# Both paged caches loaded from the SyncE queue, GpSimd left with the row stores

## The reference

```
x = x + 0.5*g1*SwiGLU_1(mod1(rmsnorm(x)))
h = mod2(rmsnorm(x)); [qA|kA|vA|qB|kB|vB|gA|gB] = h @ w_in
   branch A: block-sparse attention, 8 heads x 64, blocks of 256, top 3 past blocks + own
   branch B: differential attention, 4 heads, q/k halves of 64, value 128
   past k, v of a sample: cache[page_table[s]], 8 pages of 128 tokens x 512 values, per cache
x = x + g2*((sig(gA)*yA + sig(gB)*yB) @ w_out)
x = x + 0.5*g3*SwiGLU_2(mod3(rmsnorm(x)))
outputs: y, and the new key and value rows of both branches
```

## Time and profile before

| | |
|---|---|
| median of 3 runs | 827.73 us (826.56 to 828.61) |
| the profiled execution | 827.75 us |
| its span | 826.0 us |
| PE busy | 743.0 us (90%) |
| DVE busy | 489.2 us (59%) |
| ACT busy | 321.0 us (39%) |
| POOL busy | 82.3 us (10%) |
| bytes moved | 209.53 MB: 172.05 on q1, 36.44 on q0 |

### The profile page before, as it was taken

The page is one execution under the profiler, slowest core; times in us unless marked ns, Lnnn a source line. Parts: engine busy times, 40 slices in busy tenths (PEclk is TensorE's granted clock), DMA queues, the critical chain, the costliest instruction groups (busy, mean ns, idle before and its releaser), DMA issues. The chain is left out here.

```text
span 826.0 us, 16944 instructions
## 1 busy us (share of the span) xinstructions
PE 743.0 (90%) x6574; PEld 656.3 (79%) x6574; DVE 489.2 (59%) x663; ACT 321.0 (39%) x510; POOL 82.3 (10%) x152
## 2 busy tenths in 40 slices
PE   5589999999999988877778799979897999999997
PEld 2369898989997987767566466749787999999997
DVE  2625444445454899989995534676657545554442
ACT  2434333334333643322304533545335443544341
POOL 0000000000001202433330332300000000000000
PEclk9799999999999997999959999998898999999999
DMA  8978989897666975999993999974342565655530
GB/s 356 373 259 324 302 311 311 304 310 236 195 227 213 371 238 203 378 378 384 380 377 114 371 377 366 337 263 130 125 154 84 171 203 159 197 168 170 184 116 27
DMA packets 132903, 209.53 MB, mean 254 GB/s; under 512 B 6714, under 2 KB 100186, under 8 KB 128738
## 3 DMA queue, kind: packets, MB, share of 16 engines
q1 hardware_dynamic: 121312, 172.05, 61.1%
q0 software_dynamic: 11296, 36.44, 11.9%
q10 hardware_dynamic: 226, 0.10, 0.0%
HBM read 205.31 MB, written 3.24 MB: 253 GB/s over the span
## 5 line engine op out<-in xcount | busy, mean ns | idle before, releaser
L925 DVE TENSOR_TENSOR wlo<-raw,whi 128x1024 fp32r<-128x1024 f32 (+1 forms) x192 | 226.8, 1199 | 211.4 <-ACT whi L639 209.1
L1347 PE MATMUL bank<-hhi,whi 128*128 128x264 f32 x992 | 291.1, 293 | 18.3 <-DVE hlo L972 8.4
L1348 PE MATMUL bank<-hlo,whi 128*128 128x264 f32 x992 | 286.2, 289 | 0.0
L1349 PE MATMUL bank<-hhi,wlo 128*128 128x264 f32 x992 | 285.7, 288 | 0.0
L639 ACT ACTIVATE whi<-raw 128x1024 fp32r<-128x1024 f32 (+1 forms) x192 | 194.9, 1035 | 142.6 <-PE bank L1349 90.4
L1347 PEld LDWEIGHTS bank<-hhi,whi 128*128 128x128 f32 x992 | 192.1, 194 | 32.8 <-issue 21.6
L1348 PEld LDWEIGHTS bank<-hlo,whi 128*128 128x128 f32 x992 | 192.2, 194 | 0.2
L1349 PEld LDWEIGHTS bank<-hhi,wlo 128*128 128x128 f32 x992 | 191.1, 193 | 0.0
L1347 PE MATMUL bank<-ahi,whi 128*128 128x264 f32 x416 | 120.8, 290 | 4.0 <-DVE alo L1319 4.0
L1349 PE MATMUL bank<-ahi,wlo 128*128 128x264 f32 x416 | 119.2, 287 | 0.0
L1348 PE MATMUL bank<-alo,whi 128*128 128x264 f32 x416 | 118.9, 286 | 0.0
(11 more groups left out here) (237 smaller groups left out, 762.9 us busy)
## 6 DMA issues: line engine op xcount, KB each, us to landing
raw<-in_w_ada SPq DMA_DIRECT2D x32, 1024.0 KB, 6.9
raw<-in_ffn_w_gate SPq DMA_DIRECT2D x22, 1024.0 KB, 5.4
raw<-in_ffn_w_up SPq DMA_DIRECT2D x22, 1024.0 KB, 5.4
raw<-in_w_in SPq DMA_DIRECT2D x20, 1024.0 KB, 14.1
raw<-in_ffn_w_down SPq DMA_DIRECT2D x16, 1024.0 KB, 5.4
kvB<-in_cache_k_diff POOLq DMA_DIRECT2D x44, 256.0 KB, 6.6
kvA<-in_cache_k_moba SPq DMA_DIRECT2D x44, 256.0 KB, 9.0
kvA<-in_cache_v_moba SPq DMA_DIRECT2D x44, 256.0 KB, 6.6
```

Of the source, the lines that this page charges most:

```text
L925: dve.tensor_tensor(half_view(wlo[key[1] % 2], key, t), half_view(raw[s], key, t), half_view(whi[key[1] % 2], key, t).bitcast(F32), ALU.su ...
L1347: mm(out, wh, xh, start=start, stop=False)
L1348: mm(out, wh, xl, start=False, stop=False)
L1349: return mm(out, wl, xh, start=False, stop=stop)
```

## The change

SyncE issues the pages of both caches: for each use those of A, then those of B, then the weight tiles that AHEAD puts there. GpSimd keeps only the waits for and the stores of the rows, in the order in which the rows come (KV_BLOCKS: k0, v0, k1, v1, k2, k3, v2, v3). The register reads of `page_ids` are done by SyncE once for A and once for B. ScalarE gets a wait for the stores of all value rows ahead of the second feed-forward block, which overwrites their memory.

```
--- before.py
+++ after.py
@@ -542,14 +542,17 @@
             load_w(W_KV)
             sp.wait_ge(s_gemm, half_done(W_QK - 1, 1))
             for use in range(KVS - 1):
-                kv_load(sp, 0, use)
+                for ab in range(2):
+                    kv_load(sp, ab, use)
             load_w(W_KV + 1)
             load_w(W_KV + 2)
-            kv_load(sp, 0, KVS - 1)
+            for ab in range(2):
+                kv_load(sp, ab, KVS - 1)
             load_w(W_KV + 3)
             load_w(W_KV + 4)
             for use in range(KVS, 4 * TS):
-                kv_load(sp, 0, use)
+                for ab in range(2):
+                    kv_load(sp, ab, use)
                 if use in AHEAD:
                     for n in AHEAD[use]:
                         load_w(n)
@@ -590,9 +593,6 @@
             pool.wait_ge(s_sil, 1)
             pool.dma_start(const[:, late:NCONST], A["consts"][:, late:NCONST]).then_inc(s_const_late, 16)
             pool.wait_ge(s_gemm, half_done(W_QK - 1, 1))
-            pool.wait_ge(s_ptab, 16)
-            for use in range(KVS):
-                kv_load(pool, 1, use)
 
             def row_out(name, ab, p, src, srcs, done):
                 c0 = 256 * p
@@ -608,14 +608,11 @@
             for b in range(2):
                 ins = nc.gpsimd.memset(qrow[b][:, :, :], 0.0)
             ins.then_inc(s_qzero, 1)
-            for use in range(KVS, 4 * TS):
-                kv_load(pool, 1, use)
-                if use in K_ROWS:
-                    i = K_ROWS[use]
+            for kind, i in KV_BLOCKS:
+                if kind == "k":
                     pool.wait_ge(s_tok, 4 * (i + 1))
                     row_out("k", i // 2, i % 2, ktok, ktoks, s_krow)
-                if use in V_ROWS:
-                    i = V_ROWS[use]
+                else:
                     pool.wait_ge(s_vtok, 4 * (i + 1))
                     row_out("v", i // 2, i % 2, vtok, vtoks, s_vrow)
 
@@ -900,6 +897,7 @@
             squares(3, s_xup, 8)
             row_root(2)
 
+            a.wait_ge(s_vrow, 16 * 8)
             nc.scalar.activation(misc[:, 20:21], misc[:, 21:22], ACT.Silu)
             norm_hi(2)
             with a.Fori(0, NPAIR // 2) as i:
```

## The result

The changed kernel takes **838.77 us**, median of 4 runs (835.68 to 839.93), beside 828.06 us for the kernel before (826.56 to 828.61): ratio 1.0135, 95% interval 1.0107 to 1.0164. It is slower by 10.7 us, where 823.2 was forecast with a range up to 831.5. The profiled execution took 839.71 us, its span is 837.9 us, 11.9 more than before. The stages show where they went. The marks are the starts of rows in the timelines (the norm ahead of the projection, VectorE's first and last turn of a key slot, TensorE's first and last value product, VectorE's split of the attention's output, the first weight issue of the second feed-forward block).

A forecast was written before the change was run, and what follows sets the result against it. The prediction saw VectorE and DMA nearly full in the K stage, TensorE and DMA in the V stage, with cache A's pages late. Gains of 8.6 us less 4 for SyncE's pace gave 823.2 us, range 818.8 to 831.5.

The forecast's parts named there:

- what remains if SyncE keeps up: Both attention stages: one queue in order of need removes the stalls at uses 7 and 20, 8.6 us gained together.
- the old stall: V stage: TensorE waits 4.7 us for cache A's value page of use 20, as cache B took half the bandwidth.
- held back by a full queue: K stage: SyncE's four issues of use 7 took 8.56 us behind a weight tile, where free ones take 1.92.
- SyncE's pace: Both stages: SyncE needs 14.1 us per pair of uses, against VectorE's 14.4, DMA's 13.7 and TensorE's 14.0.
- I take it near nothing: Issue slots: a full queue's hold on SyncE, of unknown size up to 8.56 us per slot, costs almost nothing.
- I take the stage as VectorE's again, 2.26 us shorter: K stage: SyncE has some us in hand, so VectorE sets the pace and the stall of use 7 goes.
- its own tipping point of 14.4: K stage: SyncE becomes the bound from about 14.4 us per pair of uses, VectorE's own need.
- The V stage's sum: SyncE's issuing from 448.5 plus 3 us of holds: last page out at 539, landed at 543, 4 us given back.
- SyncE becomes the bound: Rival: the second cache's issue in even uses, behind reads and a weight, makes it slower, 833.1 us; chance 0.15.
- SyncE is the bound and the time is above 827: Sign of being wrong: VectorE waits in the K stage for `kvB` pages again and again.
- no difference: Rival: same bytes and engines, SyncE's pace takes what the order gives; within 2.5 us of 827.7; chance 0.22.
- The parts costed at nothing: ScalarE's new wait covered by 128 us, key-row stores covered by 22.11 us; weight tiles up to 1 us in range.

The follow-up runs named there:

- e1: The changed kernel, but SyncE reads the page numbers once per sample for both caches: 816.46 us, ratio 0.9877 to the kernel before.
- e3: The kernel before, but SyncE issues cache B's value pages while GpSimd keeps its key pages: 832.74 us, ratio 1.0071.
- e6: The changed kernel with the K stage's six weight tiles one use later, behind odd uses: 830.16 us, ratio 1.0027.
- e6b: The kernel of e6 run again, beside c1: 832.23 us, ratio 1.0056.
- e9: The changed kernel with page numbers read once for both caches in the K stage only: 827.53 us, ratio 1.0004.
- e7: e1 with four more page-number reads ahead of the pages of use 31 alone: 827.57 us, ratio 0.9994.
- c1: The changed kernel itself, run again beside e6b: 836.7 us, ratio 1.0105 to the kernel before.
- e4: The kernel before, with SyncE reading the page numbers twice in each even use: 828.66 us, ratio 1.0006.
- e5: The kernel before, with the weight tiles of uses 6 and 19 moved behind uses 7 and 20: 829.13 us, ratio 1.0027.
- e2: The kernel before, but SyncE issues cache B's key pages while GpSimd keeps its value pages: 832.29 us, ratio 1.0059.
- e8: e1 with the K stage's weight tiles behind odd uses: 814.78 us, ratio 0.9822.
- e8b: The kernel of e8 run again, on another chip: 817.77 us, ratio 0.9877.

## Why the prediction was wrong

**The gains were there.** Use 7 and use 20 wait for no page of A in after, and 16 products of use 20 take 2.1 us where they took 3.5. e1, in which SyncE keeps up, sizes them: the K stage is 2.3 us shorter (2.26 was forecast), the V stage 7.4 (4.66 + 1.7 = 6.4). To that comes a gain that the forecast did not have, 1.9 us ahead of the first turn. Altogether 11.7 us of span, 1.1 of them ahead of the second norm where the programs are alike, against the 8.6 of the step "what remains if SyncE keeps up". It doesn't keep up in the kernel as changed: the pages of B for use 20, forecast to be there at 466 to 468, are issued only from 466.58 to 468.60. The forecast's account of the old stall was short as well. It had 6.3 MB to move by 474.5; the windows of before give 257 GB/s in 450 to 460 and 387 in 460 to 475 us, 8.4 MB, so more lay ahead of that page than was counted. And "held back by a full queue" was read into the 8.56 us; no run shows how full the queue was.

**The step that failed is SyncE's pace.** "SyncE then needs 4 x 2.1 + 2 x 2.6 + 0.43 for a weight = 14.1 us", and the hold by a full queue: "I take it near nothing". The pair shown above needs 9.31 us for its four slots (1.88, 1.93 with its gap, 3.56, 1.94), 5.56 for the two reads and 0.64 around the weight: 15.51. A free slot was cheaper than put down (1.9, not 2.1), a read dearer (2.78, not 2.6), and the hold behind the weight, 1.5 us here and 0.7 to 1.8 behind the other five weights, is the term that was left out. Six pairs, from 323.06 to 418.20, average 15.86 us, 1.5 above VectorE's 14.4: 9.24 for the slots, 1.6 more than four free ones, and 6.62 for reads and weight, where 5.63 was forecast. Over six pairs SyncE falls 8.4 us behind its pace in e1 (86.8 us for the same stretch); 6.3 reach VectorE; that the lead of the filled slots takes up the rest is argued, not shown. So "I take the stage as VectorE's again, 2.26 us shorter" became 4.0 longer. The forecast stood only 0.3 us a pair from its own tipping point of 14.4, and a term of unknown size was set to nothing on the favourable side of it: that is the fault, more than the size of any one row.

**The V stage's sum was right in form.** Forecast: start 448.5, 87.5 us of issuing, 3 of holds, last page out at 539, landed at 543. Measured: start 453.40, last page out at 545.76, landed at 552.89. Of the 9.9 us, 4.9 are the late start, nearly all inherited from the K stage, 1.9 the pace, and 3.1 the landing (7.13 us, taken as 4). The three us of holds that were put in here were needed, and were missing one stage earlier.

**A term was missing at the end.** The sum priced late pages of the last use by their lateness alone. TensorE idles for them just ahead of a serial stretch, and from 550 to 560 us its clock is 0.54. That stretch took 15.0 us instead of 9.4 in after, e3, e6, e6b, e9 and e7, and 13.8 in c1, and e7 shows that lateness alone brings it. The 5.6 us are half of the whole loss of 10.7 us. The forecast also had only `kvB` late; 2.90 of the 3.93 us of waiting are for A's page. The prediction had charged a clock cost of 1.7 us behind the stall of use 20, and did not carry the thought to the stall that it forecast itself.

**The rival "SyncE becomes the bound"** is what happened, at the place it named: the second cache's issue in an even use, behind the reads and a weight. Its mechanism of size was not the right one (it had pages at 0.6 us throughout; they are 0.52 and held in places), and its 833.1 lacks the 5.6 us of the end. With them it would have come to 838.7, in part by chance, as its terms were not the measured ones. With VectorE in want of pages again and again, "SyncE is the bound and the time is above 827" read the new profile rightly.

**The page's rule.** The Trainium skill, page "DMA: Bandwidth & Descriptors", section "Issuing engines are not separate DMA queues", was weighed as a reason for no difference. That all DMAs share the same 16 engines fits: q1 alone reaches 380 to 383 GB/s in e1, as both queues did in before. By its second sentence, spreading issues over engines saves only sequencer time, usually small beside the transfer. Here the runs differ on both counts. The spread also decided whose pages came first: e1, with one order, is 11.4 us faster than before. That the order alone brings this is not shown, since e1 also takes the page issues off GpSimd. And the sequencer time was not small, since a 256 KB page costs 0.52 us to issue and 0.35 more for its share of the reads (5.56 us over 16 pages), against 0.68 us to move at 384 GB/s.

**The parts costed at nothing** stayed there: ScalarE's new wait, the key rows (20.90 us of cover where there were 22.11), and the weight tiles, as the stretch behind the attention is 25.8 us long in both kernels. The gain of 1.9 us ahead of the first turn fits ScalarE's waits for `raw<-in_w_in` in the projection, 5.9 us in before and none in after. It goes with the key pages' queue: the stretch is 36.7 to 36.9 us in all four kernels where GpSimd issues B's key pages (before, e3, e4, e5; ScalarE's waits are 6.3 us in e3) and 34.8 to 35.0 in all others. That GpSimd's first pages compete with these tiles is the likely reason; no run shows more than that.

What stays open is how the hold arises. The rows show that slots behind a 1 MB weight tile are issued slowly, and that with a read between it is mostly a later slot that is held; how much a queue takes before it holds the engine was not measured. Nor was it settled why the K stage at SyncE's pace varies so much, 158.4, 161.8 and 163.7 us in after, c1 and e2, where the five executions with the shared read there (e1, e7, e8, e8b, e9) lie within 151.8 to 152.1. Nor is the order of need priced apart from GpSimd's release: no run kept both queues and held B's pages back.

## What to carry to other kernels

Before DMAs are gathered on one engine, add up that engine's own time per period, with register reads and holds, and compare it to the bound; if they meet within a few per cent, the unknown terms decide, so set none of them to nothing. Look for work that the merger doubles but needn't: here one shared read of page numbers turned a loss of 10.7 us into a gain of 11.4. And price a late arrival by what runs behind it: just ahead of a serial stretch of small matmuls, a few us of idle time cost TensorE's clock here, and as much again.

## What the runs showed that was not expected

- A second read of the same eight page numbers (2.78 us of SyncE) is free in the old order (828.66 us) and worth 22 us in the new one (838.77 against 816.46).
- Lateness of 6.4 us at the last use cost 11.1 us of time (e7 against e1), of which 5.5 are the clock behind it.
- A single hardware queue moves as much as a hardware and a software queue together: 380 to 383 GB/s in 340 to 360 and 380 to 400 us (e1), against 384 and 380 before.
- Moving two weight tiles by one use moved TensorE's stall from use 20 to use 21 and left VectorE one of 2.51 us at use 5 in place of that at use 7 (e5); nothing was gained.
